# Gate and up pairs side by side: seven block products for both, with sums accumulated in PSUM, and one weight sum of each FFN2 turn made by GpSimd

## What is computed

```
def swiglu(h, w_gate, w_up, w_down):
    return (jax.nn.silu(h @ w_gate) * (h @ w_up)) @ w_down

x = x + 0.5 * gt1[:, None, :] * swiglu(modulate(rms_norm(x, norm_ffn1), sh1, sc1), ffn1_gate, ffn1_up, ffn1_down)
...                                   # convolution and linear attention in between
x = x + 0.5 * gt3[:, None, :] * swiglu(modulate(rms_norm(x, norm_ffn2), sh3, sc3), ffn2_gate, ffn2_up, ffn2_down)
```

## Time and profile before

| | us |
|---|---|
| three runs: median (lowest to highest) | 1434.01 (1432.2 to 1434.07) |
| span of the profiled execution, first to last instruction | 1432.1 |
| PE busy | 1389.1 (97%) |
| DVE busy | 977.2 (68%) |
| ACT busy | 539.3 (38%) |
| POOL busy | 80.2 (6%) |

### The profile page before, as it was taken

How to read it: one execution, slowest core, us unless ns; L and a number is a source line. 1 busy time by engine, 2 the same in 40 slices (tenths; PEclk the granted TensorE clock), 3 DMA queues, 4 the chain that set the end, 5 groups by cost and what they waited for, 6 DMA issues and landing times.

```text
span 1432.1 us, 28796 instructions
## 1 busy us (share of the span) xinstructions
PE 1389.1 (97%) x11782; PEld 1344.0 (94%) x11782; DVE 977.2 (68%) x1731; ACT 539.3 (38%) x797; POOL 80.2 (6%) x120
## 2 busy tenths in 40 slices
PE   6999999999999999999999999999999999999996
PEld 5899999999998999999899897999899999999996
DVE  6446675357547588998998997854554776456745
ACT  5423343224336222524243237422352344224433
POOL 6100000010001000000000000100000000000000
PEclk9999999999999999999999999999999999999998
DMA  9754646454364223213334453626312332323321
GB/s 322 237 177 155 205 149 206 147 168 142 103 208 142 89 88 93 89 60 104 125 128 146 136 169 127 220 91 198 104 59 74 92 117 89 114 76 106 101 77 60
DMA packets 132701, 189.49 MB, mean 132 GB/s; under 512 B 4621, under 2 KB 112545, under 8 KB 132386
## 3 DMA queue, kind: packets, MB, share of 16 engines
q1 hardware_dynamic: 111388, 112.54, 25.0%
q0 software_dynamic: 17136, 66.87, 14.0%
q10 hardware_dynamic: 4070, 8.57, 1.6%
HBM read 173.73 MB, written 15.18 MB: 132 GB/s over the span
## 4 chain that ended last, share of the span: by engine, by line
PE 84%; DVE 10%; ACT 3%; issue 2%; DMA 1%; POOL 0%; DVEq 0%; ACTq 0%
PE pu L646 51%; PE pu L828 13%; PE pu L817 11%; PE pu L660 2%; PE pg L690 2%; DVE w_lo L1680 1%; DMA work<-in_w_ada 1%; PE pg L1064 1%; ACT w_hi L1227 1%; DVE d L2106 1%; DVE w_lo L1969 1%; DVE work L2216 1%; PE pg L726 0%; DVE work L2215 0%; DVE work L2227 0%
## 5 line engine op out<-in xcount | busy, mean ns | idle before, releaser
L1680 DVE TENSOR_TENSOR w_lo<-raw,w_hi 128x1024 fp32r<-128x1024 f32 x152 | 186.1, 1225 | 255.5 <-ACT w_hi L1227 255.4
L1227 ACT CAST w_hi<-raw 128x1024 fp32r<-128x1024 f32 x152 | 158.9, 1046 | 412.0 <-PE pu L646 373.0
L646 PE MATMUL pu<-h_hi,w_hi 128*128 128x260 f32 x1408 | 288.4, 286 | 4.6 <-DVE work L2381 2.8
L646 PE MATMUL pu<-h_hi,w_lo 128*128 128x260 f32 x1408 | 284.1, 283 | 0.0
L646 PE MATMUL pu<-h_lo,w_hi 128*128 128x260 f32 x1408 | 283.3, 283 | 0.0
L646 PEld LDWEIGHTS pu<-h_hi,w_hi 128*128 128x128 f32 x1408 | 217.7, 189 | 8.7 <-DVE w_lo L1680 4.8
L646 PEld LDWEIGHTS pu<-h_hi,w_lo 128*128 128x128 f32 x1408 | 217.4, 189 | 0.0
L646 PEld LDWEIGHTS pu<-h_lo,w_hi 128*128 128x128 f32 x1408 | 217.2, 189 | 0.0
L2106 DVE SCALAR_TENSOR_TENSOR d<-u,cw,d 128x512 f32<-128x512 f32 x240 | 163.2, 745 | 0.1
L646 PE MATMUL pu<-f_hi,w_hi 128*128 128x260 f32 x704 | 142.9, 284 | 0.0
L646 PE MATMUL pu<-f_hi,w_lo 128*128 128x260 f32 x704 | 141.8, 283 | 0.0
(11 more groups left out here) (352 smaller groups left out, 2369.7 us busy)
## 6 DMA issues: line engine op xcount, KB each, us to landing
raw_a<-in_w_ada POOLq DMA_DIRECT2D x30, 1024.0 KB, 7.9
raw<-in_w_in SPq DMA_DIRECT2D x28, 1024.0 KB, 5.2
raw<-in_ffn_up SPq DMA_DIRECT2D x22, 1024.0 KB, 5.3
raw<-in_ffn_gate SPq DMA_DIRECT2D x21, 1024.0 KB, 5.3
raw<-in_ffn_down SPq DMA_DIRECT2D x16, 1024.0 KB, 5.1
gates_d<-sg ACTq DMA_DIRECT2D x24, 260.0 KB, 2.4
raw<-in_ffn_down SPq DMA_DIRECT2D x8, 768.0 KB, 4.4
work<-gates_d POOLq DMA_DIRECT2D x2, 2080.0 KB, 8.8
```

The lines of the kernel that those rows point to most:

```text
L646: last = mm(pu[p][:, e, 0:HALF], w[p][:, k, :], m[:, k, e * HALF:(e + 1) * HALF], start=(k == 0 and j == 0), stop=(k == k_tiles - 1 and j ...
L1227: nc.scalar.copy(w_hi[p][:], raw[:, slot, :, p * P:(p + 1) * P]).then_inc(s_hi, 1)
L1680: V.tensor_tensor(w_lo[p][:], raw[:, slot, :, p * P:(p + 1) * P], w_hi[p][:].bitcast(F32), ALU.subtract).then_inc(s_lo, 1)
```

## The change

A turn now has seven positions: P1, P2, P5, P6, P7, P4, P3. Each weight block is a pair, gate and up side by side (128 x 1024), and each position makes the block product for both, so up is made of seven products too: 14 x 12 = 168 matmuls. ACT's cast, DVE's subtraction and DVE's weight sums are all on 128 x 1024 now; there are two buffers instead of four, so ACT and DVE work two positions ahead.

The products P1, P6, P7 and P4 accumulate in one pair of PSUM banks: ACT copies P1, P1+P6 and P1+P6+P7 out to SBUF between them (the copies after P6 and P7 half by half). P5 and P3 accumulate in another pair (`pg[:, 2:4]`), P2 has `pu[1]`. DVE makes C11 = P1 + P2, C22 and C12 for gate and up in one operation each (128 x 2 x 260). The modulation's slabs move to other banks and come after P1. In the four turns of each FFN2 group POOL makes the weight sum of P7 instead of DVE. SP loads upper and lower input rows of the pair, each as two 512 KB loads (gate and up), instead of 1 MB of gate and 1 MB of up. The first down unit of groups 1 and 2 takes its last two k-tiles in swapped order. The load of the convolution state moves behind the end of FFN1's turns, since the weight sums now fill the buffer that it shares.

```diff
-TURN = 11
+TURN = 7
-P1, P2, P6, P5, P7, P4, P3, U0A, U0B, U1A, U1B = range(TURN)
+P1, P2, P5, P6, P7, P4, P3 = range(TURN)
...
@@ SP
+                    def rows_of(it, k2, sem):
+                        for slot, w in enumerate((wg, wu)):
+                            if it == 0 and k2 == 0:
+                                sp.wait_ge(s_lo, n0 - 2 + 2 * slot)
+                            c = r0 + 256 * it
+                            sp.dma_start(raw[:, slot, 4 * k2:4 * k2 + 4, :], cols(w, c, 4, 4 * k2 * P)).then_inc(sem, 16)
+                    for it, t in turns(which, g):
+                        if it:
+                            sp.wait_ge(s_wsum, 4 * (t - 1) + SUM_COUNT[P6])
+                            if which == 2:
+                                sp.wait_ge(s_pw, t - 2 * TURNS)
+                        rows_of(it, 0, s_raw0)
+                        if it:
+                            sp.wait_ge(s_blo, TURN * (t - 1) + P4 + 1)
+                        rows_of(it, 1, s_raw1)
                     sp.wait_ge(s_blo, TURN * t + P4 + 1)
                     load(Lin(n0), 0, cols(wd, 0, r0=r0))
@@ POOL
+            for g in (1, 2):
+                for it, t in turns(2, g):
+                    pool.wait_ge(s_raw0, 32 * (t + 1))
+                    pool.wait_ge(s_blo, TURN * (t - 1) + P7 + 1)
+                    nc.gpsimd.tensor_tensor(w_sums[:, SUM_OF[P7]], raw_blocks(0, 0), raw_blocks(1, 0), ALU.subtract
+                                            ).then_inc(s_pw, 1)
@@ PE, sums_of_blocks
+                    pe.wait_ge(s_p1, t + 1)
+                    pe.wait_ge(s_blo, j + P6 + 1)
+                    product(j + P6, a[:, 0], 0, t_hi[:, 1], t_lo[:, 1], start=False).then_inc(s_gh, 1)
+                    product(j + P6, a[:, 1], 1, t_hi[:, 1], t_lo[:, 1], start=False).then_inc(s_bd, 1)
...
@@ ACT, gate_turns
                         act.wait_ge(s_bd, TURN * t + pos + 1)
+                        if pos in (P6, P7):
+                            nc.scalar.copy(sg[:, row, HALF:N], pu[0][:, 1, 0:HALF]).then_inc(s_read, 1)
+                        if pos + 2 < TURN:
+                            blocks_hi(t, pos + 2)
+                        elif not last:
+                            blocks_hi(t + 1, pos + 2 - TURN)
...
+                            split_hi(Lin(at[f"down{which}_{g}"] + k), k, 0)
                         if pos == P1:
+                            nc.scalar.copy(halves(sg[:, 0, :]), psum(0)).then_inc(s_p1, 1)
+                            if it:
+                                hidden_hi(t - 1, it - 1, 0, 3)
...
+                        if pos == P4:
+                            act.wait_ge(s_c22, t + 1)
+                            af(gate[:, 1, 0:HALF], pu[0][:, 0, 0:HALF], ACT.Silu).then_inc(s_sg, 1)
+                            af(gate[:, 1, HALF:N], gate[:, 1, HALF:N], ACT.Silu).then_inc(s_sg, 1)
                         if pos == P3:
+                            hidden_hi(t, it, 1, 2)
                             act.wait_ge(s_c12, t + 1)
                             af(gate[:, 0, :], gate[:, 0, :], ACT.Silu).then_inc(s_sg, 1)
@@ DVE, gate_turns: the last position
                         if pos == P3:
+                            dve.wait_ge(s_u2, 2 * t + 2)
+                            V.tensor_tensor(gate_up[:, :, 2, HALF:N], halves(sg[:, 1, :]), pair_c, ALU.add
+                                            ).then_inc(s_c12, 1)
+                            if last:
+                                hidden_lo(t, it, 1, 2 * it + 1)
+                                dve.wait_ge(s_c12, t + 1)
+                                multiplied_row0(t)
+                                hidden_lo(t, it, 0, 2 * it + 2)
```

More of the change, by code:

```diff
@@ L1249, in ada_rows @@
                 act.wait_ge(s_ad, m.value(1, 1))
[L1250 removed]
+                nc.scalar.copy(rows_a[:, slot], pg[:, slot, 0:256]).then_inc(s_ar, 1)
             def late_rows(g):
@@ L1417, in ffn @@
                             step(n, False)
-                            for b in range(2):
-                                block_hi(*next(turns(which, g + 1)), 2 * (c - 6) + b)
+                            blocks_hi(next(turns(which, g + 1))[1], c - 6)
                         else:
@@ new lines, in gate_turns @@
+                        if pos == P4:
+                            dve.wait_ge(s_c22, t + 1)
+                            dve.wait_ge(s_sg, 3 * t + 1)
+                            V.tensor_tensor(gate[:, 1, 0:HALF], gate[:, 1, 0:HALF], pu[0][:, 1, 0:HALF], ALU.mult
+                                            ).then_inc(s_um, 1)
+                        if pos == P3 and not last:
+                            add_weights(t + 1, P5)
+                        if pos + 2 < TURN:
+                            blocks_lo(t, pos + 2)
+                        elif not last:
+                            blocks_lo(t + 1, pos + 2 - TURN)
+                        else:
+                            k = pos - P4
+                            split_lo(Lin(at[f"down{which}_{g}"] + k), k, 0)
@@ L1991, in gate_turns @@
+                        if pos == P6 and not last:
+                            add_weights(t + 1, P7)
                         if pos == P4:
-                            dve.wait_ge(s_u3, t + 1)
-                            V.tensor_tensor(sg[:, 1, 0:HALF], u3, bank[1], ALU.add).then_inc(s_c2, 1)
+                            dve.wait_ge(s_sg, 3 * t + 2)
+                            V.tensor_tensor(gate[:, 1, HALF:N], gate[:, 1, HALF:N], up[:, 1, HALF:N], ALU.mult
+                                            ).then_inc(s_um, 1)
+                            ada_part(2, ADA_UP[g] + 2 * it, None)
@@ L2059, in ffn @@
                         if g < 2 and c >= 6:
-                            it, t = next(turns(which, g + 1))
+                            t = next(turns(which, g + 1))[1]
                             step(n, False)
-                            for b in range(2):
-                                block_lo(it, t, 2 * (c - 6) + b)
+                            residual(n, c, gt)
+                            blocks_lo(t, c - 6)
+                            add_weights(t, P7 if c == 6 else P5)
                         else:
                             step(n, n0 + c + 2 < UNITS)
-                        residual(n, c, gt)
+                            residual(n, c, gt)
                         if which == 2 and g == 2:
@@ L2070, in ffn @@
                             scale_of(SCF, "norm_final")
-                        if g < 2 and c in (5, 6):
-                            t = next(turns(which, g + 1))[1]
-                            add_weights(t, 2 * (c - 5))
-                            add_weights(t, 2 * (c - 5) + 1)
                         if g == 2 and c:
```

321 lines of the change are left out of this document (164 added, 157 removed).

## The result

The changed kernel takes 1466.3 us (median of four, 1465.7 to 1468.3) against 1434.0: a ratio of 1.023, interval 1.0217 to 1.0246. The profiled run took 1468.3, 2.0 more than the median; its span is 1466.4, 34.3 longer than the span before.

The account below looks back on a forecast made before the run. It took the turns to be PE-bound. Removed work -23.8, waits in turns +20.1, set ends +20.8 and clock +6.2 gave +23.3 on the median of 1434.0: 1457 us, range 1443 to 1470.

Parts of the forecast that it names:

- Removed, -23.8: 12 fewer matmuls in each of 16 turns, 23.0 us, and two waits before the first P6, 0.8 us.
- Waits in the turns, +20.1: PE waits for weight blocks: 1.55 us per FFN2 turn, 2.0 or 0.6 in FFN1's, 3.0 in all first turns.
- rival 1: DVE stands still for POOL's sum: 0.6 us in each of six running FFN2 turns, 3.6 in all, 1461; chance 0.22.
- The end of a set, +20.8: First down unit waits 5.2 us, four times, for the lower hidden tile's split, queued behind late-loaded down weights.
- the upper bound: At the ends of the sets: 25.4 us if one of four loads takes the 9.7 us seen beside POOL's.
- The clock, +6.2: After each of the four end waits PE runs at granted clock 0.50, costing 1.55 us each; from 0 to 12.
- POOL's sum, 0: POOL's P7 weight sum, about 2.5 us, is wanted five positions later, so off the path: costs 0.
- rival 3: Lower weight rows land late: 1.2 us in five turns beside modulation loads, 4.6 at one end; 10.6, so 1468; chance 0.10.
- Half the waits: In the turns, pieces overlap a little better and ten of the twenty us go: 1447; chance 0.15.
- PE-bound: Each position's chain fits in 2.69 us everywhere, only the ends remain, no clock loss: faster, 1426; chance 0.12.
- The margin of 0.1 us: Per position, the chain of cast and subtraction alone takes 2.58 us of 2.69, if neither engine has anything in front.

Follow-up runs that it names:

- the halved subtraction: Against the changed kernel, DVE makes the lower half of each weight block for the gate alone (128 x 512 instead of 128 x 1024): 1439.2 us.
- the turns in another order: Against the changed kernel, in running turns only, pieces standing in front of a block's cast or subtraction go behind it; GpSimd's sum stays: 1453.3 us.
- all orders together: Against the changed kernel, set ends and running turns reordered, and DVE makes GpSimd's sum at the end of position P7: 1428.5 us, ratio 0.9958.

## Why the prediction was right, and where it was short

It said slower, 1457 and 1443 to 1470; measured, 1466.3. By its own steps:

- *Removed, -23.8*: right within 1 us, by the halved subtraction.
- *Waits in the turns, +20.1*: measured 24.6 inside the sets and 1.55 ahead of FFN2's first. The turns of FFN1 were right: with modulation 0.56 to 0.70 longer than with the halved subtraction (0.6 predicted), without it 2.15 (2.0). FFN2's running turn is 2.17 longer than with the halved subtraction, not 1.55. A wait of PE costs about 0.25 more than its idle time: the last product's tail of 0.28 - 0.12 still counts as busy, and the second matmul comes 0.19 to 0.23 instead of 0.12 after the first. Counted so, from the starts of the matmuls, P5 costs 0.33 (0.35 predicted), P6 0.61 (0.6), P1 0.59 (0.4) and P4 0.65, for which the sum held no more than a share of the 0.2 for P7, P4 and P3; the rest stood in rival 1. The four make the 2.17. In working out P5 and P6 the prediction took some 0.03 between cast and subtraction, not its own 0.11, which would have made 0.43 and 0.69; the trace shows 0.03 there (P5's cast ends at 1192.23, the subtraction starts at 1192.26). That the order makes the waits at P5, P6 and P1 is shown by the turns in another order.
- *The end of a set, +20.8*: 22.5, in the row that was named; 5.1 in FFN2, 5.8 and 6.4 in FFN1. The order made them, and behind it the load. FFN1's second end is the longest, and its first load the late one, 6.5 us where the other three take 5.1 to 5.2, though not beside GpSimd's loads, as the upper bound had it: these were issued as it landed.
- *The clock, +6.2*: right in kind, and 7.2 by the trace. The parts behind the first, third and fourth ends are 2.0, 1.3 and 1.4 us longer than before, and with short waits they are not. Behind the second, 34 matmuls run in the first 6.1 us where the kernel before has 55: 21 x 0.12 = 2.5 us. The price of one wait was read too high: the earlier trace rows give 28 - 18 = 10 matmuls of 0.12, 1.2 us, not 1.5. Behind the second end the granted clock stayed at 0.50, the lower of its two levels, for 4.8 us (406.9 to 411.7).
- *POOL's sum, 0*: this step failed. Rival 1, given 0.22, was right in its mechanism and near in its 0.6 a turn (1.72 - 1.22 = 0.50 as DVE shows it, and 0.76 with the new turn order). It missed the start of the first set, where PE waits 1.55 us and with the sum on DVE 0.38. P4 costs 0.65 a turn beside GpSimd's sum and 0.16 without it, so six turns and that start make some 4 of the excess of 9 us over 1457. DVE's relief was no more than the loss: with the sum on DVE the turn is as long, because P3 then waits.

The Trainium skill, "SBUF — State Buffer", section "Who interferes with whom", says that a DVE instruction with two SBUF inputs and a GpSimd one that reads SBUF shut each other out for a whole instruction. The trace agrees: DVE's ends stand 1.09, 1.07 and 0.56 us behind the ends of POOL's (1202.38, 1165.01, 1206.54), about its own duration later. Made twice, GpSimd's sum stretched DVE further; given back to DVE, it stretched nothing. So the rule bore on this case.

- *Late weights, rival 3*: true for two loads inside the sets, 1.47 us in FFN1's first turn and 0.70 in FFN2's last, and in part for the load at FFN1's second end.
- *Half the waits, and PE-bound*: wrong. The margin of 0.1 us was as thin as worked out.

With 24.6 + 1.55 + 22.5 + 7.2 - 23.8 = 32.05, some 2 of the span's 34.3 us are left. 1.5 stand ahead of the first set, whose first product starts between 155.98 and 157.01 us in kernels with the same code up to there; the rest is of the size of the tails that count as busy ahead of the five long waits (0.16 each). Against the forecast's terms that is 6.1 more in the turns, POOL's share included, 1.7 more at the ends and 1.0 more for the clock.

## What to carry to other kernels

When fewer matmuls leave less time per block of work, list for each block what stands in front of its cast and its subtraction in the queues: here the saving of 23.8 us was real, and orders written for a longer position, with a sum on GpSimd and a clock that fell behind the waits, gave back more than it. The same products in another order, the sum on DVE and the down weights loaded earlier, make a kernel that is 1.0% faster than the kernel before. At the end of a set put first what doesn't wait for a load, and load early the rows whose slots are free early. Look at what DVE does beside an element-by-element operation before handing it to GpSimd: here, beside subtractions with both inputs in SBUF, it was no relief.

## What the runs showed of the hardware

- GpSimd's 128 x 1024 subtraction takes 2.40 us against DVE's 1.22. It is stretched as well when they meet: 2.73 with the new turn order, and 5.75 for two.
- The clock kept 1.00 behind waits of 1.65 to 1.78 us at the ends of the sets, and fell to 0.50, 1.2 GHz, behind 3.48 and more. With all orders together it fell behind 1.83 (0.50 from 1232.6 to 1235.8 us) and 3.25 as well, and in the kernel before behind 1.98.
